# Three narrow projections in two passes with buffers of their own, rotary halves exchanged by DMA, and four reorderings on VectorE

## The reference

```python
mod = silu(c) @ w_ada + b_ada                 # six groups of 1024
h = rms_norm(x, g) * (1 + sc1) + sh1
# first block
q_a, k_a, v_a, q_d, k_d, v_d, z_d, b_d, a_d = split(h @ w_in)   # b_d, a_d: 8 columns each
y = concat(dilated_attention(q_a, k_a, v_a), gated_deltanet(q_d, k_d, v_d, z_d, b_d, a_d)) @ w_out
# second kind, twice
a_q, a_ff, a_fb, a_i, a_g, b_q, b_k, b_v, b_g, c_q, c_k, c_v, c_g, c_lr, gates = split(h @ w_in)  # c_lr: 32 columns
f = lb + (1 - lb) * sigmoid(a_ff); key = (1 - lb) * sigmoid(-a_ff)       # forget gates, and so backward
o_a = bidirectional_scan(silu(a_q), key_f, key_b, a_i, log f_f, log f_b)
o_b = bidirectional_scan(rotary(b_q), rotary(b_k) / 8, ..., constant decay)
o_c = bidirectional_scan(c_q / 8, c_k, ..., log_sigmoid(c_lr @ w_alpha + b_alpha) / 16)
merged = sum of sigmoid(gate) * (y @ w_p) over a, b, c;  y = merged @ w_out
# both: x += g1 * y; h = rms_norm(x) * (1 + sc2) + sh2; x += g2 * (silu(h @ w_gate) * (h @ w_up)) @ w_down
```

## Time and profile before

| | |
|---|---|
| runs | 2824.12, 2828.1, 2830.7 us |
| profiled execution | 2826.71 us |
| its span | 2824.8 us |
| TensorE busy | 2739.8 us, 97% |
| VectorE busy | 1440.8 us, 51% |
| ScalarE busy | 1134.9 us, 40% |
| POOL busy | 216.6 us, 8% |
| DMA | 306.85 MB, mean 109 GB/s |

### The profile page before, as it was taken

The page is one execution under the profiler, slowest core; times in us unless marked ns, Lnnn a source line. Parts: engine busy times, 40 slices in busy tenths (PEclk is TensorE's granted clock), DMA queues, the critical chain, the costliest instruction groups (busy, mean ns, idle before and its releaser), DMA issues.

```text
span 2824.8 us, 39217 instructions
## 1 busy us (share of the span) xinstructions
PE 2739.8 (97%) x16750; PEld 2181.2 (77%) x16750; DVE 1440.8 (51%) x1888; ACT 1134.9 (40%) x1395; POOL 216.6 (8%) x196
## 2 busy tenths in 40 slices
PE   6998889999999999999999999999999999999998
PEld 4876878888877777677788888887776777888886
DVE  6485657443466664445673444555543355633322
ACT  4375244222244533446442222355425454432221
POOL 0011301000021100001010001010100010100001
PEclk8999999999999999999999999999999999999999
DMA  6531014433332132232234334321231222232221
GB/s 255 195 132 57 4 61 158 162 137 129 123 134 75 61 141 106 74 131 73 110 140 158 137 143 142 116 90 68 94 128 46 77 78 73 90 105 96 94 97 56
DMA packets 46245, 306.85 MB, mean 109 GB/s; under 512 B 5455, under 2 KB 6351, under 8 KB 12792
## 3 DMA queue, kind: packets, MB, share of 16 engines
q1 hardware_dynamic: 44584, 296.95, 28.9%
q0 software_dynamic: 1488, 7.39, 0.8%
HBM read 302.21 MB, written 2.12 MB: 108 GB/s over the span
## 4 chain that ended last, share of the span: by engine, by line
PE 48%; ACT 1%; DVE 1%; issue 0%; ACTq 0%; DVEq 0%
PE bank L2307 40%; PE bank L2239 3%; PE bank L2290 1%; PE bank L2658 1%; PE bank L2629 1%; PE bank L2787 0%; PE bank L2644 0%; PE bank L2674 0%; PE bank L2327 0%; PE bank L2360 0%; DVE ost L1692 0%; PE bank L2638 0%; PE bank L2782 0%; PE bank L2733 0%; ACT WH L978 0%
## 5 line engine op out<-in xcount | busy, mean ns | idle before, releaser
L2307 PE MATMUL bank<-HH,WH 128*128 128x512 f32 x2232 | 899.6, 403 | 11.1 <-DVE HL L1687 5.7
L2307 PE MATMUL bank<-HH,WL 128*128 128x512 f32 x2232 | 871.3, 390 | 0.0
L2307 PE MATMUL bank<-HL,WH 128*128 128x512 f32 x2232 | 871.0, 390 | 0.0
L1569 DVE TENSOR_TENSOR WL<-raw,WH 128x2048 fp32r<-128x2048 f32 (+4 forms) x266 | 485.2, 1830 | 590.4 <-ACT WH L978 589.8
L978 ACT ACTIVATE WH<-raw 128x2048 fp32r<-128x2048 f32 (+3 forms) x223 | 396.0, 1776 | 343.6 <-PE bank L2307 305.5
L2307 PEld LDWEIGHTS bank<-HH,WH 128*128 128x128 f32 x2232 | 417.9, 187 | 122.1 <-issue 23.1
L2307 PEld LDWEIGHTS bank<-HL,WH 128*128 128x128 f32 x2232 | 418.3, 187 | 93.5 <-issue 8.9
L2307 PEld LDWEIGHTS bank<-HH,WL 128*128 128x128 f32 x2232 | 417.8, 187 | 91.2
L2307 PE MATMUL bank<-AH,WH 128*128 128x512 f32 x492 | 191.4, 389 | 0.0
L2307 PE MATMUL bank<-AH,WL 128*128 128x512 f32 x492 | 191.4, 389 | 0.0
L2307 PE MATMUL bank<-AL,WH 128*128 128x512 f32 x492 | 191.4, 389 | 0.0
(11 more groups left out here) (396 smaller groups left out, 3434.5 us busy)
## 6 DMA issues: line engine op xcount, KB each, us to landing
raw<-in_wstream_dram SPq DMA_DIRECT2D x256, 1024.0 KB, 4.9
raw<-in_wstream_dram SPq DMA_DIRECT2D x24, 512.0 KB, 3.5
raw<-in_wstream_dram SPq DMA_DIRECT2D x12, 768.0 KB, 4.2
bgam<-in_consts_dram POOLq DMA_DIRECT2D x2, 1792.0 KB, 7.1
xT<-in_x_dram SPq DMA_DIRECT2D x2, 1024.0 KB, 7.6
out_dram<-ost SPq DMA_DIRECT2D x4, 512.0 KB, 2.7
toep<-bias_dram POOLq DMA_DIRECT2D x6, 256.0 KB, 3.8
ctab<-in_cond_dram SPq DMA_DIRECT2D x2, 512.0 KB, 4.4
```

Of the source, the lines that this page charges most:

```text
L1569: TT(WL[:, wi % 2, now], raw[:, j.load % RAW, now], WH[:, wi % 2, now].bitcast(F32), ALU.subtract).then_inc(s["w_split"], 2 if half is Non ...
L2307: last = MM(o[m][0:cw, :], a, b, start=j.first and u == 0 and q == 0, stop=j.last and u == j.units - 1 and q == 2)
```

## The change

1. The narrow projections are no longer jobs of the stream. `narrow` steps round and split a small tensor `wlow` (128 x 8 x 32, loaded by POOL) into `narrow_hl`, with the high and the low part side by side: 64 columns. `low` steps make 16 matmuls with HH and HL against it (four products where there were three); the two halves of the 64 output rows are summed by the next matmul, since `choose` and `walpha` now have their rows twice. `low` of the layers stands between cq and ck, so ck stands between it and decay.
2. The rotary's halves are exchanged by four DMAs of POOL (32 partitions of 8 KB each) from `bqk` (bq and bk in one tensor) to `bturn`; the sign is in the sine table. VectorE then makes three operations of 2048. TensorE has no part in it.
3. `forget` of head 0 goes ahead of the split of the job av (both layers).
4. `merge` follows its pc job directly; a modulation chunk that belongs behind that job comes behind the merge. Since three jobs less are counted or stand in the list, the modulation chunks from the c part of layer 1 on move to later places.
5. Some semaphores are joined (`halves_in` into `c_in`, `lb_max` and `g_square` into `dve_start`).

```diff
     for i, kind in enumerate(IN1):
+        if i == 5:
+            steps.append(("narrow", 0))
         if i == 6:
-            job("ba", 0, 0)
+            steps.append(("low", 0))
             steps.append(("gates", 0))
...
-        for kind, c in (("gb", 2), ("pb", 0), ("pb", 1), ("cq", 0), ("ck", 0), ("cl", 0)):
+        for kind, c in (("gb", 2), ("pb", 0), ("pb", 1)):
             job(kind, L, c)
+        steps.append(("narrow", L))
+        job("cq", L, 0)
+        steps.append(("low", L))
+        job("ck", L, 0)
         steps.append(("decay", L, 0))
...
         for c in range(4):
+            at = len(steps) + 1
             job("pc", L, c)
-            steps.append(("merge", L, c))
+            steps.insert(at, ("merge", L, c))
...
-    blocks["sin"] = np.sin(ang)[p % 32]
+    blocks["sin"] = np.sin(ang)[p % 32] * np.where(p % 64 < 32, -1.0, 1.0)[:, None]
...
+                if st[:2] == ("job", "bv") and st[3] == 0:
+                    pool.wait_ge(s["act_evac"], evacuated("bk", st[2], 0))
+                    for a in range(0, P, 32):
+                        pool.dma_start(bturn[a:a + 32, :, :], bqk[a ^ 32:(a ^ 32) + 32, :, :]).then_inc(s["r_rot"], 16)
...
                 elif st[0] == "job":
                     if n not in EMBEDDED:
+                        if st[1] == "av":
+                            forget(st[2], 0)
                         if STEPS[n - 1][0] != "decay" and n not in SPLIT_EARLY:
                             begin(n)
                         end(n)
...
-                        if st[1] == "av":
-                            forget(st[2], 0)
...
-                    dve.wait_ge(s["r_in"], 64 * (r + 1))
-                    for x in range(4):
...
-                        TT(btmp[:, :], bank[4 + x][:, :], brot[:, S:2 * S], ALU.mult).then_inc(s["r_t"], 1)
-                        TT(t, t, brot[:, 0:S], ALU.mult).then_inc(s["r_t"], 1)
...
+                    dve.wait_ge(s["r_rot"], 64 * (r + 1))
+                    TT(bturn[:, :, :], bturn[:, :, :], bc(brot[:, S:2 * S], [0, 4], [1, S]), ALU.mult).then_inc(s["r_t"], 1)
+                    TT(bqk[:, :, :], bqk[:, :, :], bc(brot[:, 0:S], [0, 4], [1, S]), ALU.mult).then_inc(s["r_t"], 1)
+                    dve.wait_ge(s["r_t"], 3 * r + 2)
+                    TT(bqk[:, :, :], bqk[:, :, :], bturn[:, :, :], ALU.add).then_inc(s["r_t"], 1)
...
+            def narrow(layer):
+
+                o = bank[5 if layer else 7]
+                for u in range(KD):
+                    for q, x in enumerate((HH, HL)):
+                        last = MM(o[0:64, :], narrow_hl[min(layer, 1)][:, u, :, :], x[:, u, :], start=u == 0 and q == 0,
+                                  stop=u == KD - 1 and q == 1)
+                last.then_inc(s["l_done"], 1)
```

More of the change, by code:

```diff
@@ L90, in job @@
         whole = kind != "down" or i % 3 == 2
-        chunk = whole and (kind == "down" or sum(x[0] == "job" for x in steps + [("job",)]) % every == 0)
+        chunk = whole and (kind == "down" or sum(x[0] in ("job", "low") for x in steps + [("job",)]) % every == 0)
         if chunk and (kind, i) in LAST_OUT:
@@ L350, in constants @@
     for h in range(8):
-        choose[h, 8 * (h % 2) + h // 2] = choose[8 + h, 8 * (h % 2) + 4 + h // 2] = 1.0
+        for g in (0, 32):
+            choose[g + h, 8 * (h % 2) + h // 2] = choose[g + 8 + h, 8 * (h % 2) + 4 + h // 2] = 1.0
     blocks["choose"] = choose
@@ L1120, in evacuate @@
                         put(zs[:, 2 * (i - 12) + m, :], o[m][:, :], ACT.Silu)
-                elif kind == "ba":
-                    put(CO[0:16, 11, :], o[0][0:16, :])
                 elif kind == "gate":
@@ L1170, in evacuate @@
                             scale=0.125 if kind == "cq" else 1.0)
-                elif kind == "cl":
-                    put(clr[0:32, :], o[0][0:32, :])
                 elif kind == "cv":
@@ L1462, in _ @@
                             begin(after_short(n))
+                elif st[0] == "narrow":
+                    act.wait_ge(s["c_in"], 32 + 32 * st[1] if st[1] else 16)
+                    A(narrow_hl[min(st[1], 1)][:, :, 0, :], narrow_raw[min(st[1], 1)][:, :, :], ACT.Copy).then_inc(s["l_split"], 1)
+                elif st[0] == "low":
+                    act.wait_ge(s["l_done"], st[1] + 1)
+                    A(clr[0:64, :] if st[1] else CO[0:64, 11, :], bank[5 if st[1] else 7][0:64, :], ACT.Copy
+                      ).then_inc(s["l_out"], 1)
                 elif st[0] == "gates":
@@ L2193, in _ @@
                         if i == 0:
[L2194 removed]
+                            dve.wait_ge(s["r_in"], 48 * layer)
                         e = i % 2
@@ L2302, in gemm @@
                         pe.wait_ge(s["h_low"], heads_done(n) - 4 + u + 1)
-                    for m in range(2 if wd == CW else 1):
-                        wh, wl = (x[:, sl, u * wd + P * m:u * wd + P * m + cw] for x in (WH, WL))
+                    for m in range(2):
+                        wh, wl = (x[:, sl, u * wd + P * m:u * wd + P * m + P] for x in (WH, WL))
                         xh, xl = (x[:, k0 + u, :] for x in X)
                         for q, (a, b) in enumerate(((wh, xh), (wh, xl), (wl, xh))):
-                            last = MM(o[m][0:cw, :], a, b, start=j.first and u == 0 and q == 0,
+                            last = MM(o[m][:, :], a, b, start=j.first and u == 0 and q == 0,
                                       stop=j.last and u == j.units - 1 and q == 2)
@@ L2700, in _ @@
                     pe.wait_ge(s["bias_rows"], 2)
-                    pe.wait_ge(s["act_evac"], evacuated("ba", 0, 0))
+                    pe.wait_ge(s["l_out"], 1)
                     for n in range(8):
                         for e in range(2):
-                            last = MM(bank[6][64 * e:64 * e + 64, 8 * n:8 * n + 8], CO[0:16, 11, chunk(n)],
-                                      choose[0:16, 8 * e:8 * e + 8], start=True, stop=True)
+                            last = MM(bank[6][64 * e:64 * e + 64, 8 * n:8 * n + 8], CO[0:64, 11, chunk(n)],
+                                      choose[0:64, 8 * e:8 * e + 8], start=True, stop=True)
                     last.then_inc(s["ba_turned"], 1)
@@ L2751, in _ @@
                         gemm(n)
+                elif st[0] == "low":
+                    pe.wait_ge(s["l_split"], 2 * st[1] + 2)
+                    pe.wait_ge(s["bias_rows"], 2)
+                    pe.wait_ge(s["h_low"], heads_done(n))
+                    narrow(st[1])
                 elif st[0] == "attn":
@@ L2755, in _ @@
                     delta()
-                elif st[0] == "rotary":
-                    r = st[1] - 1
-                    js = [JOBS[m] for m in range(n) if STEPS[m][0] == "job" and STEPS[m][1] == "bk"]
-                    pe.wait_ge(s["act_evac"], js[-1].act)
-                    pe.wait_ge(s["r_in"], 64 * (r + 1))
-                    pe.wait_ge(s["h_low"], heads_done(n))
-                    for x in range(4):
-                        t = (bq if x < 2 else bk)[:, x % 2, :]
-                        MM(bank[4 + x][:, :], brot[:, 2 * S:2 * S + P], t, start=True, stop=True
-                           ).then_inc(s["r_rot"], 1)
                 elif st[0] == "mix":
@@ L2771, in _ @@
                         if i == 0:
-                            pe.wait_ge(s["r_t"], 12 * layer)
+                            pe.wait_ge(s["r_t"], 3 * layer)
                         if e == 0:
```

92 lines of the change are left out of this document (44 added, 48 removed).

## The result

The changed kernel takes **2808.36 us** (median of four runs, 2808.03 to 2809.04), the kernel before 2829.4 in the same comparison (2824.12 to 2831.06): a ratio of 0.9929, 95% interval 0.9917 to 0.9941. The forecast was 2809.4 with a range of 2804.5 to 2815.0. The profiled execution has a span of 2806.2 us, 18.6 less than before; the sum of the prediction was 18.7. The total is right almost to the microsecond, but one of its terms is not, and 2.6 us come from stretches where I had nothing, as the rest shows.

A forecast was written before the change was run, and what follows sets the result against it. The prediction took TensorE's back-to-back matmuls as the bound, so only removed matmuls or TensorE waits pay. Terms 5.6 + 1.4 + 6.9 + 4.2 + 0.6 = 18.7 us, from 2828.1 to 2809.4 us, range 2804.5 to 2815.

The forecast's parts named there:

- Narrow jobs and clr: Three narrow projections at 16 matmuls instead of 24, 5.6 us off; the 0.7 us copy wait before decay gone twice, 1.4 us.
- Rotary: Between the bv job and bg in each layer: its matmuls leave TensorE, 2 x 3.44 = 6.9 us off.
- about 1080: Predicted landing time of the rotary exchange in us, middle of 1077.9 to 1083.6; needed by 1086.7.
- the exchange makes it slower: Rival at the rotary: SBUF to SBUF transfer so slow that scores wait; landing 30 us after the copy gives 2846.6; chance 3%.
- Forget gates: First scan of layer 1: gates ahead of the weight split, level 1 starts at 849.2 instead of 853.47, 4.2 us off.
- The wait that is left is 842.0 to 845.5: TensorE's remaining wait at the first scan of layer 1, for POOL's adds; full clock was assumed behind it.
- my 845.5: Predicted end of POOL's adds at the first scan of layer 1, when the matmul over eadd starts, instead of 848.03.
- the late bound of 846.5: Latest predicted end of POOL's adds, if each moved gate operation and the split block POOL for its length.
- Half clock stays: Rival at the first scan: TensorE waits over 3.5 us, clock 0.50 again, 4.2 us shrink to 2: 2811.6; chance 13%.
- Merge: Wait for HL before the output projection: HL ready at 1412.0 instead of 1412.6, 0.6 us off, bounds 0 and 2.8.
- The merge pays in full: Rival at the merge: the late load isn't in the path, 2.1 us off instead of 0.6: 2807.9; chance 10%.
- 2.8 us did no harm: Argument against the half clock rival: after the 2.8 us wait at 1412 the granted clock stayed at 1.00.

## Why the prediction was right, and where it wasn't

- **Narrow jobs and clr, 7.0 us: right.** 1.77, 2.59 and 2.55 us, 6.9 in all; the matmuls took 3.68 us each as forecast. What the step missed is the price of a short wait in clock, 1.47 us behind the decay of layer 2, and the new wait for WL in block 1, a loss of 1.1 us.
- **Rotary, 6.9 us: right**, 3.43 and 3.17. The landing came 7.0 us after the first issue, near the middle of the bounds; on the time line of before that is 1079.8, where the prediction has "about 1080". The slack of 7 us was read rightly too: the exchange issued 11 us late costs 4.3 us of wait in each layer. The rival in which the exchange makes it slower has its mechanism (the wait and then a lowered clock: 4.3 + 2.95 us), but nothing moves as slowly as it would need.
- **Forget gates, 4.2 us: wrong, 1.76.** The step that failed is "The wait that is left is 842.0 to 845.5, between these two and nearer the second; I take full clock." The adds ended at 843.62, which is 846.2 on the time line of before (2.6 us later), 0.7 past my 845.5 and next to the late bound of 846.5. The wait was 4.2 us, and 0.63 was granted behind it. From level 0's start to that of the eadd matmul 5.3 us against 4.5 forecast, and from there to level 1 5.4 against 3.7: together 2.5 us, all of the miss. This was the rival *Half clock stays*, at 13%, and it is what happened. The term's lower bound of 2 us was the better number.
- The adds are slow for the reason given: VectorE's operations and POOL's adds lengthen one another (1.79 against 0.68 for the same gate operation, 3.37 against 2.29 for the split; six adds in 11.88 us where one alone takes 1.29). What the step left out is the modulation chunk behind the split. With the gates gone from there it comes 3 us earlier and meets the last add. The last add of the changed kernel and that of the kernel before:

```profile
841.57 2.06 POOL L858 TENSOR_TENSOR eadd<-eadd,esq 128x512 f32<-128x512 f32 x1
...
843.37 1.53 POOL L859 TENSOR_TENSOR eadd<-eadd,esq 128x512 f32<-128x512 f32 x1
```

Row by row the six adds lose 0.8 us to the gate operations (0.2 before), 1.8 to the split (the same before) and 0.8 to the chunk (none before). My 0.6 us for the moved gates was right; the 0.7 us by which 845.5 was missed is the chunk. No run moved the chunk alone in the changed kernel, so this is read from the rows of one trace and not tested. By the Trainium skill's page "SBUF — State Buffer" (Who interferes with whom), one of the two blocks the other for a whole instruction; the trace agrees, in both directions. Moving VectorE's work earlier moved it onto the adds: the gates, and behind them the chunk.
- **Merge, 0.6 us: right**, 0.75, and for the reason given: the load of the second output job. With the chunk ahead of merge 1 again ScalarE's wait goes from 2.01 to 0.87 and TensorE's from 1.85 to 0.67. That is 2.1 us less than the 2.80 before, the number of the rival *The merge pays in full*, which asked for a load that isn't in the path: there it isn't.
- **The rows I leaned on for the clock.** "Against: 2.8 us did no harm" rests on one execution. Three of the four traces with that wait show a lowered clock behind it. One profile can't say what a wait costs when the cost is there in some executions only.
- **The total** is right by luck: 2.4 us too much at the first scan stand against 2.6 us that I had nowhere. These are the clock behind a decay (1.47), the start and the c scans (0.3 each), and 0.49 in which 1.65 us of clock in the middle stages hide a loss of 1.1. The changed kernel's second profile shows how loose such numbers are: its span is 0.9 us longer, 1.0 of it from the attention of the first block, where the granted clock stood at 0.50 for 3.4 us and in the first profile didn't.
- That the median moved more than the span (21.0 against 18.6) fits this too: the profiled execution of before, 2826.71 us, is below the median of its runs (2829.4), and the runs of before scatter over 7 us, those of the changed kernel over 3. A kernel with fewer short waits has fewer places at which the clock can fall. That this is why the scatter shrank is argued from the counts, not shown run by run.

## What to carry to other kernels

Price a wait of TensorE with what the clock does behind it, and look at more than one execution before calling a wait harmless: here a wait of 0.7 us ahead of the decays cost 0.7 in half of the cases and 2.2 in the other half, and no clock fell behind the waits of 0.6 to 1.6 us that were counted at two other places. When an operation is moved earlier, ask what shares a resource with it there and who is next in line: the gates came in time, but they and the chunk behind them pushed POOL's adds, and the wait stayed under another name until POOL's own order was changed. Where the gain of a part is smaller than the scatter of whole runs, read it from the start of the same instruction in both traces, place by place.

## What the hardware showed

- Behind a wait of 0.7 us ahead of the decays the granted clock went to 0.50 for some 3.4 us in five of ten cases, at a cost of about 1.5 us each, and a wait of 1.6 us in block 1 was followed by no such fall in 14 traces. I had expected nothing of so short a wait.
- Four pieces of 256 KB from SBUF to SBUF land 7.0 us after the first is issued, 4.3 us each by the median: near the 4.9 us of the 1 MB loads of weights and not slower.
- Four adds of POOL took 12.04, 7.76 or 6.91 us by what VectorE did beside them; four times the one that ran alone is 5.2. The loss goes both ways: the same modulation operation of VectorE takes 1.22 us alone and 2.28 to 2.31 beside an add.
